# Decode rows of q and k first, prompt rows as three fp32r products, in a two-layer decoder step

## What is computed

```python
q, k, v, z, xbc, dt = jnp.split(x @ w_in, IN_SPLITS, axis=-1)      # x: tokens x 1024
q = _rope(q.reshape(b, L, 2 * ATT_HEADS, ATT_QK_DIM), pos)         # 512 columns
k = _rope(k.reshape(b, L, 2 * ATT_HEADS, ATT_QK_DIM), pos)         # 512 columns
s = jnp.einsum('bqhmd,bkhmd->bhmqk', q, k_all) * scale             # decode: k_all holds the cached keys
conv = conv_b + sum(xbc_pad[:, i:i + L] * conv_w[i] for i in range(CONV_WIDTH))
dt = jax.nn.softplus(dt + dt_bias)
acs = jnp.cumsum(dtc * a_head, axis=2)                             # decays
```

## Time and profile before

| | us |
|---|---|
| three runs | 1755.17, 1757.46, 1763.50 (median 1757.46) |
| the profiled execution | 1755.76 |
| its span in the trace | 1753.8 |
| start of layer 0: decode rows of q to the end of the last `qb` | 18.77 to 93.23 |
| the same in layer 1 | 592.73 to 666.68 |

### The profile page before, as it was taken

The page is one execution under the profiler, slowest core; times in us unless marked ns, Lnnn a source line. Parts: engine busy times, 40 slices in busy tenths (PEclk is TensorE's granted clock), DMA queues, the critical chain, the costliest instruction groups (busy, mean ns, idle before and its releaser), DMA issues.

```text
span 1753.8 us, 22732 instructions
## 1 busy us (share of the span) xinstructions
PE 1707.6 (97%) x8473; PEld 1325.7 (76%) x8473; DVE 1183.2 (67%) x1522; ACT 810.0 (46%) x844; POOL 156.3 (9%) x141
## 2 busy tenths in 40 slices
PE   7999999899999999999989999999999999999997
PEld 4645487689999765548768888888888888888885
DVE  2687524445543358763443698888998989899986
ACT  1122211134442212221112477777777777777774
POOL 0540000000000054000001300000000000000001
PEclk9999999999999999999999899999999999999999
DMA  9566542765544446654276498999999999999993
GB/s 323 198 205 217 216 188 107 272 208 192 169 145 145 148 149 213 216 216 186 108 277 227 164 370 293 389 381 379 385 375 389 377 393 373 390 373 392 372 394 120
DMA packets 220577, 466.18 MB, mean 266 GB/s; under 512 B 11135, under 2 KB 50233, under 8 KB 220487
## 3 DMA queue, kind: packets, MB, share of 16 engines
q1 hardware_dynamic: 213446, 444.76, 70.0%
q0 software_dynamic: 4752, 16.25, 3.2%
q10 hardware_dynamic: 2304, 4.20, 0.6%
HBM read 447.10 MB, written 18.21 MB: 265 GB/s over the span
## 4 chain that ended last, share of the span: by engine, by line
PE 90%; DVE 6%; ACT 2%; issue 1%; SPq 1%; DMA 1%; ACTq 0%; DVEq 0%
PE bank L1268 87%; PE bank L1272 3%; DVE arena L2723 1%; DMA out<-mem_rows 0%; ACT arena L1884 0%; DVE R L2337 0%; DVE arena L2826 0%; DVE st L2695 0%; SPq L733 0%; ACT SQ L1905 0%; DVE pair_in L2356 0%; SPq L739 0%; ACT xT L1920 0%; DVE arena L2703 0%; DMA wr<-in_w_router 0%
## 5 line engine op out<-in xcount | busy, mean ns | idle before, releaser
L2202 DVE TENSOR_TENSOR ring_low<-ring,high 128x2048 fp32r<-128x2048 f32 x264 | 600.9, 2290 | 81.8 <-ACT high L1819 81.4
L1819 ACT ACTIVATE high<-ring 128x2048 fp32r<-128x2048 f32 x264 | 506.6, 1919 | 150.4 <-PE bank L1268 142.7
L1268 PE MATMUL bank<-high,xg_high 128*128 128x512 f32 x704 | 278.0, 395 | 0.0
L1268 PE MATMUL bank<-ring_low,xg_high 128*128 128x512 f32 x704 | 275.0, 391 | 0.0
L1268 PE MATMUL bank<-high,xg_low 128*128 128x512 f32 x704 | 274.7, 390 | 0.0
L1268 PEld LDWEIGHTS bank<-ring_low,xg_high 128*128 128x128 f32 x704 | 132.6, 188 | 28.2
L1268 PEld LDWEIGHTS bank<-high,xg_high 128*128 128x128 f32 x704 | 132.6, 188 | 27.1
L1268 PEld LDWEIGHTS bank<-high,xg_low 128*128 128x128 f32 x704 | 132.7, 189 | 26.5
L1884 ACT ACTIVATE arena<-bank 128x512 f32<-128x512 f32 (+3 forms) x89 | 43.1, 521 | 210.9 <-PE bank L1268 141.4
L1268 PE MATMUL bank<-high,he_high 128*128 128x512 f32 x352 | 139.1, 395 | 0.0
L1268 PE MATMUL bank<-ring_low,he_high 128*128 128x512 f32 x352 | 137.2, 390 | 0.0
(11 more groups left out here) (327 smaller groups left out, 2442.4 us busy)
## 6 DMA issues: line engine op xcount, KB each, us to landing
ring<-in_w_exp_gu SPq DMA_DIRECT2D x176, 1024.0 KB, 14.0
ring<-in_w_exp_down SPq DMA_DIRECT2D x40, 2048.0 KB, 16.1
ring<-in_w_in SPq DMA_DIRECT2D x12, 2048.0 KB, 11.2
ring<-in_w_ffn_gu SPq DMA_DIRECT2D x22, 1024.0 KB, 8.4
ring<-in_w_ckv SPq DMA_DIRECT2D x8, 2048.0 KB, 8.3
ring<-in_cache_mem_k SPq DMA_DIRECT2D x16, 1024.0 KB, 8.2
ring<-in_cache_mem_v SPq DMA_DIRECT2D x16, 1024.0 KB, 6.7
ring<-in_cache_attn_k SPq DMA_DIRECT2D x32, 256.0 KB, 4.3
```

The costliest lines, as they stand in the source:

```text
L1268: return M.matmul(out, lhsT, rhs, start=start, stop=stop)
L1819: S.activation(high_bufs[h % HIGH_BUFS][:], ring[:, s, j * HALF:(j + 1) * HALF], ACT.Copy).then_inc(split_high, 1)
L2202: V.tensor_tensor(ring_low[:, s, part], ring[:, s, part], high_bufs[h % HIGH_BUFS][:], ALU.subtract).then_inc(split_low, 1)
```

## The change

- The decode rows of q, `dt`, and the decode rows of k now come first on PE.
- The prompt rows of q and k are computed by `prompt_rows` as three fp32r products. ACT rounds each weight half of 128x2048 into one of two buffers `tok_high_bufs` (`tok_high_part`), DVE writes the rest in place over the ring (`tok_low_part`), ACT rounds the input into `xq_high` (eight pieces), and DVE writes `xq_low` (eight pieces).
- `acs` stands between q and k, ahead of the `qb` group; the eight `qb` stand among k's products (two ahead, four between, two behind), and no longer among the convolution blocks. On DVE all eight `cached_scores` run ahead of the first convolution block. Since two banks of k are open while four `qb` finish, `PsumTurns` gets an order of finishing beside the order of opening.
- `scT` stands ahead of the fifth convolution block, and its load is issued by POOL behind the rotations.
- POOL rotates the decode rows first (all 16 heads), then q and k of the prompt apart (8 heads each, with the same six operations on half the width).
- The small loads (`dt_bias`, `a_log`, `d_skip`, `lambda_params` and the dt columns of layer 0) are issued by POOL at its start, and the dt columns of layer 1 and the router weights by POOL behind the decode rotation of layer 0. SP loads K0 and K1 ahead of xbc0 and xbc1.

```diff
+        add("V", "tok", "q", 2)
+        add("V", "dt")
+        add("V", "tok", "k", 2)
         for c in ("q", "k"):
...
+            for t in range(2):
+                add("A", "tok", c, t)
+            if c == "q":
+                add("V", "acs")
+                for b in range(2):
+                    add("V", "qb", b)
+            else:
+                for b in range(2, 8):
+                    add("V", "qb", b)
...
+                def prompt_rows(c, between):
...
+                    for j in range(2):
+                        pe.wait_ge(tok_high, tok_half(l, c, j) + 1)
+                        high = tok_high_bufs[j].rearrange("p (k n) -> p k n", k=4)
+                        for t in range(2):
+                            for kk in range(4):
+                                k = 4 * j + kk
...
+                                mm(bks[t][:], xq_high[:, k, t * P:(t + 1) * P], high[:, kk, :], k == 0, False)
+                            for kk in range(4):
+                                k = 4 * j + kk
...
+                                last = mm(bks[t][:], xq_low[:, k, t * P:(t + 1) * P], high[:, kk, :], False, False)
+                            if t:
+                                last.then_inc(tok_high_used, 1)
+                            if between:
+                                cached_row(2 + 2 * j + t)
+                    for t in range(2):
+                        for k in range(KT):
+                            if t == 0 and k % 4 == 0:
+                                pe.wait_ge(tok_low, tok_half(l, c, k // 4) + 1)
+                            last = mm(bks[t][:], xq_high[:, k, t * P:(t + 1) * P], low[:, k, :], False, k == KT - 1)
+                        full(last)
...
+            def tok_high_part(l, c, j):
+
+                s, n = rg.arrived(act, (l, c)), tok_half(l, c, j)
+                if c == "k":
+                    act.wait_ge(tok_high_used, n - 1)
+                    act.wait_ge(tok_low, n - 1)
+                S.activation(tok_high_bufs[j][:], ring[:, s, j * HALF:(j + 1) * HALF], ACT.Copy).then_inc(tok_high, 1)
...
+                if (l, i) == (0, 2):
+                    passed(act, (0, "d", 7))
+                    for j in range(2):
+                        tok_high_part(1, "q", j)
...
                 other_quarters(1, "k", qk_raw[0:8, 2, 512:1024])
...
+                for j in range(2):
+                    tok_low_part("q", j)
+                rope_ready.wait(dve, l, 0)
+                split_rows(qkr[0:8, 2, 0:512], pair_q).then_inc(pair_ready.sem, 1)
```

More of the change, by code:

```diff
@@ L145, with __init__ @@
 class PsumTurns:
-    def __init__(self, groups, banks, full, emptied):
+    def __init__(self, groups, finished, banks, full, emptied):
         self.groups, self.banks, self.full, self.emptied = groups, banks, full, emptied
         self.index = {g: n for n, (g, _) in enumerate(groups)}
+        self.place = {g: n for n, g in enumerate(finished)}
+        assert set(self.place) == set(self.index)
         seen = {k: 0 for k in emptied}
@@ L169, in take @@
     def take(self, eng, name):
[L171 to L173 removed]
+        eng.wait_ge(self.full, self.place[name] + 1)
+        return self.banks[self.index[name] % len(self.banks)]
     def passed(self, eng, name):
[L177 removed]
+        eng.wait_ge(self.full, self.place[name] + 1)
     def copied(self, eng, name):
@@ L730, in _ @@
                 columns((l, "q"), w_in, 0)
[L731 to L743, removed]
+                columns((l, "k"), w_in, 512)
                 if l == 0:
@@ L747, in _ @@
                     pages((l, "K", i), a["cache_attn_k"][l], 4 * i)
-                for key, c0 in (("v", 1024), ("z", 1536)):
+                for key, c0 in (("xbc0", 2048), ("xbc1", 2560), ("v", 1024), ("z", 1536)):
                     columns((l, key), w_in, c0)
@@ L1433, in _ @@
+                full(last)
+                token_major("k", 2)
+                prompt_rows("q", False)
                 bk = turns.open(pe, (l, "acs"))
@@ L1439, in _ @@
                 full(last)
-                bk = turns.open(pe, (l, "scT"))
-                pe.wait_ge(conv_state_landed, 16 * (l + 1))
-                for m in range(8):
-                    last = tr(bk[:, 24 * m:24 * m + 24], sc_in[:, m * P:(m + 1) * P], 24)
-                full(last)
+                for b in range(2):
+                    cached_row(b)
+                prompt_rows("k", True)
+                for b in range(6, 8):
+                    cached_row(b)
                 for b in range(8):
@@ L1448, in _ @@
                     block_of(w, (l, "xbc"), b, xT)
-                    bk = turns.open(pe, (l, "qb", b))
-                    if b == 0:
-                        pair_ready.wait(pe, l)
-                    full(on_all(bk, b, pair_in))
+                    if b == 4:
+                        bk = turns.open(pe, (l, "scT"))
+                        pe.wait_ge(conv_state_landed, 16 * (l + 1))
+                        for m in range(8):
+                            last = tr(bk[:, 24 * m:24 * m + 24], sc_in[:, m * P:(m + 1) * P], 24)
+                        full(last)
                     if b == 0:
@@ L1921, in norm @@
                                  ).then_inc(xT_act.sem, 1)
+                if (l, i) == (0, 2):
+                    for k in range(KT):
+                        scaled.wait(act, l, 8 * i + k)
+                        S.activation(xq_high[:, k, :], R[:, k, :], ACT.Identity, bias=col_b(l, i, k)
+                                     ).then_inc(xq_high_ready.sem, 1)
             S.preload_act_table_set(EXP_AND_LN)
@@ L2377, in _ @@
             decode_columns(0)
-            dve.wait_ge(small_landed, 16 * 9)
+            for k in range(KT):
+                xq_high_ready.wait(dve, 0, k)
+                V.tensor_tensor(xq_low[:, k, :], xT[:, k, :], xq_high[:, k, :], ALU.subtract
+                                ).then_inc(xq_low_ready.sem, 1)
+            dve.wait_ge(small_landed, 16 * 7)
             step.inc(V.tensor_tensor(lprod[:, :, 0, :], lraw[:, :, 0, :], lraw[:, :, 1, :], ALU.mult))
```

185 lines of the change are left out of this document (124 added, 61 removed).

## The result

| kernel | median, us | runs, us | profiled span, us |
|---|---|---|---|
| before | 1756.9 | 1751.5 to 1763.5 | 1753.8 |
| after | 1761.9 | 1759.0 to 1768.8 | 1759.5 |

The ratio after to before is 1.0042, 95% interval 1.0029 to 1.0054. That is 7 us longer by the ratio and 5.0 us by the medians. The interval leaves out "no change", but the difference is smaller than the spread of either kernel's runs. The forecast was 1759 (1745 to 1767). The change saves 10 of the 11.7 us that it promised on the products, and loses more than that in one place, which exists twice.

The account below looks back on a forecast made before the run. PE was taken to bound the kernel, busy for 90% of the chain. Layer 1's +0.2 and layer 0's +2.6 us sum to +2.8 on the profiled execution's 1755.76 us, giving 1759 us, range 1745 to 1767.

Parts of the forecast that it names:

- 13.7 for k and the rows: PE after the wait: 48 products of k at 0.2275 us and eight `qb` at 0.36 us take 13.7 us.
- Products: q's and k's prompt rows on PE: 10.92 us per matrix instead of 13.84, saving 11.7 us at most over four.
- Hold-up of the rotation: DVE's two 128x2048 weight pieces exclude POOL's rotation of decode rows, 4.2 us per layer; bounds 0 and 4.6.
- the list of signs: What the changed profile would show; here, two of POOL's six rotation operations 3.3 us long instead of 1.26.
- The rival without exclusion: First rival: DVE's weight pieces and POOL's rotation run side by side, no clock loss; 1746 us, chance 0.2.
- The wait: PE ahead of the first `qb` waits for the split of q's decode rows: 4.7 us in layer 1.
- The exponentials: Set-up on ACT in layer 0, behind input pieces and weight halves: start at about 25.2, one at about 25.5.
- The clock again: At the start of k, behind PE's wait, the granted clock drops: 1.67 us lost, bounds 0 and twice that.
- Convolution blocks: Convolution stage on PE: eight blocks at 3.83 us make 30.6, with `dtb` and `scT` 32.3 us.
- The start: Small loads leave SP's queue; if their packets delay x and mem, up to 1 us is allowed.
- Third rival: Convolution state lands late behind POOL's 24 half-width operations, PE waits at `scT`: 1772 us, or 1781; chance 0.07.
- The norm between the layers: ACT's two weight halves, 3.8 us, fit its 11.97 us idle before its first square; costed at nothing, bounds 0 and 3.8.

Follow-up runs that it names:

- the last kernel but one: Changed kernel with all eight cached rows behind k's prompt rows, small loads back on SP, k's low pieces ahead of the rotation wait: 1737.5 us, ratio 0.9901.
- the filled kernel: Changed kernel with ten float32 products of no use put ahead of PE's wait for the split of q: 1751.3 us, ratio 0.9985.
- the pieces first: Changed kernel with q's two low pieces on DVE ahead of the adding up of k's decode rows: 1757.3 us, ratio 1.0007.
- the loads on SP: Changed kernel with the seven small loads of the start issued by SP behind q's columns again: 1758.3 us, ratio 1.0013.
- The kernel with float32 products: Changed kernel's order with q's and k's prompt rows as float32 products again, splits still made but not read: 1760.5 us, ratio 1.0035.

## Why the prediction came out as it did

Its time was 3 us short of the median and its sign right, but that is partly luck. The clock and k's interleaved products cost 9.7 us more than forecast, and the convolution blocks and a store outside the changed stages gave 6.6 back. Of the 3 us, 1.7 are no term of the mechanism: the prediction names them as the distance from the profiled execution to the median and leaves them out; with them its terms give 1760. (Its 13.7 for k and the rows should be 13.8, from 10.92 + 2.88, and its 1.1 for `dtb` 1.0. The two nearly cancel.)

- **Products: right in kind, 15% too good.** 10.92 us per matrix were taken from the experts; q took 11.28, k in one piece 11.34. Four times 2.5 to 2.6 is 10, not 11.7. What was left out: k's products with a cached row in every eight take longer still. With the clock up, k and eight rows take 15.19 us so, and 11.34 + 2.05 = 13.4 in one piece. The interleaving costs 1.8 us a layer, and the prediction's 13.7 had no such term.
- **Hold-up of the rotation: right.** 4.2 us were taken, 4.1 measured (5.40 - 1.28). It is not two operations of 3.3 us, as the list of signs said, but one of 5.4: DVE's second piece started before GpSimd got in. Both forms are to be seen beside the four pieces of the last kernel but one (5.41, 3.31, 3.21). The rule of the Trainium skill, "SBUF — State Buffer", section "Who interferes with whom", by which DVE and GpSimd exclude each other there, is borne out for long operations too, with 1.28 against 5.40 us. The rival without exclusion (1746) falls.
- **The wait: right.** 4.7 us in layer 1 were forecast, 4.49 came. The row 0 product was forecast for 619.2 and started at 620.97, of which 1.9 is the late start of the layer. In layer 0 it was 48.1 against 48.45. The exponentials stood at 26.0 to 26.2, not 25.2 to 25.5.
- **Clock: the term that was mis-sized.** "The clock again" gave the start of k what the start of q pays behind `dt`, 1.67 us, with bounds of 0 and 3.3. It was 4.1 and 6.0 us, outside the bounds, 6.7 us too little in sum. The price of one stretch was carried to another with other work in it. Behind `dt` the level was back after 3.4 us; here it took 9.3 and 13.7. That the idle time brings the low clock was right, as the filled kernel shows. That the price can't be read off one execution is shown by the two kernels that kept the rows in place: the same stretch cost 2.4 and 4.3 us with the pieces first, and 2.2 and 4.4 us with the loads on SP, in layer 0 within the forecast's bounds.
- **Convolution blocks: the cancelling miss.** Eight blocks were costed by the length of one row, 3.83 us. Without a row between them they start 3.6 us apart (in layer 1 64 products, four blocks, run for 14.51 us in one row). 30.6 us were taken, 32.3 forecast: 1.7 us a layer, 3.4 in all.
- **The start: outside its allowance.** Up to 1 us was allowed for the small loads' effect on x, and x came 3.2 us later (12.97 against 9.79). The chain of layer 0 still came out within 0.4 us of the forecast, and that is luck. The 40 transposes behind x took 6.26 us, where they had taken 8.22 before and took 8.1 to 8.2 in five of the variants and 5.9 to 6.2 in three; the granted clock stands at 1.00 there in the traces of the kernels before and after alike, so the cause stays open. With the slow ones the filled kernel's split came 1.6 us later.
- **What was made good later** (3.2 us at the store of layer 0) was in no step. The kernel with float32 products, which reaches that place later still, lost what the kernel before loses there; the filled one made good what the changed one does. It is a matter of where a store meets other transfers, and it wasn't tested by itself.
- **Third rival** (the convolution state): the half-width operations on GpSimd took 0.73 us where no DVE operation held them, below the 0.92 from which it was to decide. `scT` shows no wait. It stands behind the fifth block and not, as the text ahead of the result says, in front of it: in the kernel its products follow those of block 4, counted from 0. In layer 1:

```profile
646.95 14.51 PE L1310 MATMUL bank<-xT,ring 128*128 128x264 f32 x64
661.39 0.67 PE L1314 MATMUL bank<-const,SQ 24*128 24x24 f32 x8
```

One block (642.15) lies ahead of these four. The load, issued at 649.88, took 6.6 us and so was there 4.9 us early. With the right place the point from which the rival decides is 1.08 us an operation, not 0.92. The norm between the layers was not lengthened: ScalarE's first square found 0.59 us of its 11.97 us of idle time left.

By the terms: 2.8 forecast; clock +6.7, k's products among the rows +3.0 (15.2 for 13.7, twice), blocks -3.4, and the waits +0.2, make +9.3, and that is layer 0's 5.1 and layer 1's 4.2. Less 3.2 at the store and 0.4 at the end, it is the 5.7 us between the spans.

## What to carry to other kernels

A wait of TensorE ahead of k cost its own length here (1.5 to 6.7 us) and then a slow stretch behind it, whose loss (1.7 to 6.0 us) may be larger than the wait; waits of 1.0 us within q and k brought none. So when a chain over DVE and GpSimd feeds a small product, put the large products that don't need it between the last thing they share and that product, and look for the free place on TensorE before shortening the chain: here moving eight small products was worth 20 us, while unlocking the chain was worth some 5. And cost a run of equal blocks by the distance of their starts, not by the length of one.

## What the hardware showed that was not expected

- The lower clock level lasted 3.4 and 6.1 us (float32 products, 1.46 and 3.68 us of idle time before), 5.1 us twice (fp32r in one piece, 3.6 and 3.9 us before) and 5.2 to 13.7 us (fp32r with small products between, 2.4 to 6.7 us before), with TensorE busy throughout by the trace. The length of the idle time does not order them: 6.66 us cost 2.4 us of clock and 2.43 us cost 4.3.
- 4.6 us of products with no use, in place of the idle time, were worth 10.6 us.
- A GpSimd operation of 1.28 us took 5.40 beside two DVE operations back to back: DVE's next one can start before the waiting engine is let in.
- On GpSimd an operation of 128 by 256 took 0.73 us, and one of 512 columns 1.26 us on 8 partitions as on 128 (627.38 us of the kernel before): its time went by the width, not by the partitions.
- Seven small loads from GpSimd's queue at the start made x land 3.1 us later (12.97 us) than the same loads issued behind q's columns on SP (9.83 us).
